# First block's gates as pairs of column chunks with seven-product units, and another order of the bank reads at the ends of output pairs

## The chip, the cores and the metric

One core of one Trainium2 chip. The metric is the device time of one execution in microseconds (us), given as the median of three runs.

## The reference

Two transformer-like blocks run one after the other on an activation of 256 tokens by 2048 channels, in fp32. What the change touches:

```python
# first block
proj = rms_norm(x, norm_mix_g) @ w_in              # the last 4 * 2048 columns are the gates
gates = sigmoid(gate_logits.reshape(b, s, 4, d))   # one gate of 2048 columns for each of four branches
branches = einsum('bskw,kwd->bskd', ys, w_branch)
merged = sum(gates * branches, axis=2)
x = x + merged @ w_out
x = x + square(relu(rms_norm(x, norm_mlp_g) @ w_mlp_up)) @ w_mlp_down
# second block
...
x = x + (silu(h2 @ w_gate) * (h2 @ w_up)) @ w_down
```

## The kernel before

**Products.** Every large product is fp32 made of three passes of a reduced type (fp32r): each operand is split into a high half (a rounded copy) and a low half (the rest), and high x high, low x high and high x low are added in PSUM. ACT makes the high half of the weights (`hi_unit`, L422), DVE the low half (`lo_unit`, L430), both for a unit of 1 MB. Weights pass through a ring of four raw slots and two split slots. A unit is four k-tiles by 512 columns; with two row tiles of 128 tokens it has 24 matmuls of 512 columns (`unit_products`, L433 to L456): sixteen that need the high half, then eight that need the low half. Semaphores order everything: `hi_split` and `lo_split` count halves of units, `units_used` the units that PE has done. ACT makes the high half of a unit when PE has done the unit two before; SP loads a unit when the low half of the one three before is made.

**Order.** PE runs 76 groups of four units and then the units of the pairs of the second block. Groups 8 to 11 are the gates of four branches for the first chunk of 512 columns, group 12 the four branch products for it. Groups 13 to 27 are three turns of five groups for the other three chunks (`gate_turn`, L1673): one group for each branch's gate, accumulated in `acc[:, k % 2]`, and one group of four branch units. ACT turns a gate into a sigmoid when its group is done (`evac`, L958), while PE works in the other half of `acc`. DVE multiplies gate and branch (`branch_part`, L2171, instruction L2182) and POOL adds the four results (`merge`, L899). Turned matrices pass through the PSUM tile `tp` (L500) on the way to the output product. Groups 28 to 31 are w_out, 32 to 35 the first up product.

**Pairs.** From group 36 on, three times, come two output pairs ("scaled") and four up groups; the second block's MLP consists of pairs too: 11 of gate and up, 6 of down. A pair works on two chunks of columns at once, so on all four banks of `acc` (chunk b, row tile m). Its unit is two k-tiles by two chunks: a 2 x 2 x 2 product of blocks. Units 3 and 5 (in the first down pairs others) are done with seven products instead of eight, by sums of blocks: `seven_low` and `seven_high` make the sums of weight blocks and split them (DVE L2272 to L2286, ACT L987 to L992), `operand_sums` and `operand_low` (L2289 to L2310) with `sums_high` (L994) make those of the other operand, once for an operand. `seven_products` (L1743) has 21 matmuls. Three of the seven products go to banks of their own in `sd` and `tp`; `combine` (L2325) makes vw and yz from them after the last seven unit and q_sum is copied by ACT (`q_copy`, L1003). `plain_products` (L1706) does the first and the last unit of a pair bank by bank: in the first it waits for each bank to be free (`bank_free`, L1691), does four matmuls, waits for the whole low half, and does two more. In the last each bank reports when it is done (`bank_done`).

**Ends of output pairs.** After the first unit's split of the next pair (or the up group), DVE runs `finish_scaled` (L2378): the two banks of chunk 0 into xres (`bank_to_x`, L2350), then the combined sums into xres (`sums_to_x`, four operations at L2364), then the two banks of chunk 1. In the second block `finish_first` and `finish` (L2596, L2605) do the same with L2352 and L2371 to L2375. After a gate pair the first addition (L2603) is made before the next unit's split already.

Of the kernel before, what the change touches and what calls it, by code (L numbers as in the profile page):

```python
# [110 lines left out]
FIRST_SEVEN, QUARTERS = (3, 5), 3  # L111

# [13 lines left out]
def build(nc, t, out):  # L126

    ctx = ExitStack()
    with ctx:
# [132 lines left out]
        t_sum = at("t_sum", 160, [P, 4, NW])  # L262
# [3 lines left out]
        a_full = at("a_full", 164, [P, 2, T])  # L266
        a_sum = at("a_sum", 166, [P, 4, P])
# [4 lines left out]
        q_sums = [at("q_sum", 148, [P, NW]), at("q_sum2", c0 + 1.5, [P, NW])]  # L272
# [83 lines left out]
        q_copied = sem("q_copied")  # L356
        combined, silu_in, hidden2 = sem("combined"), sem("silu_in"), sem("hidden2")
# [28 lines left out]
        w_dn = rows_of(t["w_mlp_down"][0])  # L386
        conv_cols = t["w_in_2"][0][:, I2_B0:I2_B0 + 2 * W].rearrange("(k p) (v f n) -> p k v f n", p=P, v=2, f=2)
# [11 lines left out]
        def loads_before(group):  # L399

            return group + min(max(group - G_HEAD2, 0), 2) + max(group - G_PAIR0, 0)
# [134 lines left out]

        PAIRS1 = [Pair(n, "scaled", (G_DLOOP + 8 * (n // 2)) * UN + n % 2 * PAIR_UNITS, PAIR_UNITS, FIRST_SEVEN, 1,
# [14 lines left out]
        for p in PAIRS1 + PAIRS:  # L552
            ahead = PAIRS1[:p.n] if p.kind == "scaled" else PAIRS1 + PAIRS[:p.n]
            p.order = len(ahead)
            p.combined = sum(3 if q.kind == "gate" else 6 for q in ahead)
# [3 lines left out]
            p.q_sum = q_sums[p.kind != "scaled"]  # L559
# [11 lines left out]
        SUMS1 = 2 * QUARTERS  # L571
# [7 lines left out]
        SUM_LOWS = [last_seven(PAIRS1[2 * i], 0) for i in range(QUARTERS) for _ in range(2)]  # L579
# [6 lines left out]
        def sums_made(p, v):  # L586

            x = p.places.index(v)
            if p.kind == "scaled":
                return 2 * p.chunk[0] + x + 1  # L590
            return SUMS1 + (x + 1 if p.op == 0 else 3 + 2 * p.chunk[0] + x)

# [102 lines left out]
        def _(sp):  # L695
# [262 lines left out]
        def _(act):  # L958
# [22 lines left out]
            def seven_high(p, v):  # L981
# [8 lines left out]
                act.activation(seven_hi[:, 3:5, :], t_sum[:, 0:2, :], ACT.Copy)  # L990
                act.wait_ge(t_made, 3 * n + 3)
                act.activation(seven_hi[:, 5:7, :], t_sum[:, 2:4, :], ACT.Copy).then_inc(hi_split, 1)  # L992
# [5 lines left out]
            def first_sums_high(i, j):  # L998

                if j in (1, 3):  # L1000
                    sums_high(1, j // 2, 2 * i + j // 2)
# [1670 lines left out]
```

## Time and profile before

| | us |
|---|---|
| median of 3 runs (2473.68 to 2473.72) | 2473.7 |
| the profiled execution | 2474.51 |
| its span, first to last instruction | 2472.8 |
| PE busy | 2453.8 |
| PE weight loads busy | 2047.9 |
| DVE busy | 1708.5 |
| ACT busy | 1212.2 |
| POOL busy | 116.6 |

Matmuls are pipelined: one of 512 columns is shown with some 390 ns, though the next starts some 227 ns after it. So the pace is read from starts, not from durations. The waits view names for each idle time of an engine the instruction that ended it. In a timeline row stand start, duration, engine, line, operation, output and inputs, a count where neighbours are merged, and in brackets the idle time before it and what ended it.

### The profile page before, as it was taken

To read this page: it belongs to the slowest core of one execution; us is meant where nothing else is said; L and a number is where in the kernel's file an instruction comes from. 1 tells how busy PE (TensorE), PEld (TensorE's weight loads), DVE (VectorE), ACT (ScalarE), POOL (GpSimd) and SP (SyncE) were. 2 spreads that over 40 slices of the span, in tenths; PEclk is the share of its full clock that TensorE was granted. 3 is DMA by queue.
4 is the path that set the end of the run, shared out by engine and by line. 5 is a ranking of instruction groups with operands and counts; after the bars stand their busy time and mean duration, and the time that the engine had idled before them with its cause. 6 is when DMAs were issued, how large, how long until landed. Compare 5 with 4: busy or idle time off the path is not lost.

```text
span 2472.8 us, 28758 instructions
## 1 busy us (share of the span) xinstructions
PE 2453.8 (99%) x11719; PEld 2047.9 (83%) x11719; DVE 1708.5 (69%) x1590; ACT 1212.2 (49%) x1270; POOL 116.6 (5%) x95
## 2 busy tenths in 40 slices
PE   9999999999999999999999999999999999999999
PEld 8888888888888878888888888788888788878887
DVE  5775455454655785776765558886788878887887
ACT  5545534343344444544444448875555444544553
POOL 0410010010110000000000010000200000000000
PEclk9999999999999999999999999999999999999999
DMA  7555465666655565655665655444556565655654
GB/s 252 173 184 180 160 192 192 196 194 196 230 184 187 187 201 188 197 192 175 201 194 192 209 171 189 153 151 162 180 191 199 190 194 185 207 195 191 203 187 153
DMA packets 233138, 467.18 MB, mean 189 GB/s; under 512 B 13424, under 2 KB 25216, under 8 KB 232622
## 3 DMA queue, kind: packets, MB, share of 16 engines
q1 hardware_dynamic: 231454, 460.09, 57.4%
q10 hardware_dynamic: 1552, 5.25, 0.6%
q8 instruction: 93, 1.52, 0.3%
q14 instruction: 39, 0.32, 0.0%
HBM read 463.20 MB, written 2.10 MB: 188 GB/s over the span
## 4 chain that ended last, share of the span: by engine, by line
PE 93%; DVE 4%; ACT 1%; issue 1%; POOL 0%; DMA 0%; ACTq 0%; DVEq 0%; POOLq 0%
PE acc L445 13%; PE acc L454 13%; PE acc L447 13%; PE acc L1714 9%; PE acc L1715 9%; PE acc L1718 9%; PE acc L474 5%; PE acc L480 2%; PE sd L474 2%; PE tp L474 2%; DVE wlo L430 1%; PE tp L480 1%; PE sd L480 1%; PE acc L1772 1%; PE acc L1768 1%; PE acc L1769 1%
## 5 line engine op out<-in xcount | busy, mean ns | idle before, releaser
L430 DVE TENSOR_TENSOR wlo<-raw,whi 128x2048 fp32r<-128x2048 f32 (+1 forms) x396 | 913.5, 2308 | 642.9 <-ACT whi L422 641.8
L422 ACT ACTIVATE whi<-raw 128x2048 fp32r<-128x2048 f32 (+1 forms) x396 | 748.0, 1890 | 844.4 <-PE acc L454 356.4
L445 PE MATMUL acc<-whi,opA_hi 128*128 128x512 f32 x1152 | 454.8, 395 | 0.0
L447 PE MATMUL acc<-whi,opA_lo 128*128 128x512 f32 x1152 | 449.4, 390 | 0.0
L454 PE MATMUL acc<-wlo,opA_hi 128*128 128x512 f32 x1152 | 287.4, 391 | 0.2 <-DVE wlo L430 0.2
L445 PEld LDWEIGHTS acc<-whi,opA_hi 128*128 128x128 f32 x1152 | 216.9, 188 | 45.4 <-issue 0.9
L447 PEld LDWEIGHTS acc<-whi,opA_lo 128*128 128x128 f32 x1152 | 216.8, 188 | 44.2
L454 PEld LDWEIGHTS acc<-wlo,opA_hi 128*128 128x128 f32 x1152 | 214.9, 188 | 44.8 <-DVE wlo L430 0.8
L1714 PE MATMUL acc<-whi,opA_hi 128*128 128x512 f32 x552 | 216.0, 391 | 5.9 <-DVE xres L2350 3.8
L1715 PE MATMUL acc<-whi,opA_lo 128*128 128x512 f32 x552 | 215.0, 389 | 0.0
L1714 PE MATMUL acc<-whi,opB 128*128 128x512 f32 x536 | 209.7, 391 | 1.4 <-DVE xres L2352 1.4
L1715 PE MATMUL acc<-whi,opB 128*128 128x512 f32 x536 | 208.7, 389 | 0.0
L474 PE MATMUL acc<-opB,whi 128*128 128x512 f32 x512 | 159.2, 392 | 1.1 <-DVE xres L2350 1.1
L445 PE MATMUL acc<-whi,opB 128*128 128x512 f32 (+1 forms) x384 | 147.5, 387 | 2.0 <-ACT whi L422 2.0
L1718 PE MATMUL acc<-wlo,opA_hi 128*128 128x512 f32 x552 | 148.1, 389 | 0.0
L447 PE MATMUL acc<-whi,opB 128*128 128x512 f32 (+1 forms) x384 | 145.1, 381 | 0.0
L1718 PE MATMUL acc<-wlo,opB 128*128 128x512 f32 x536 | 143.1, 389 | 0.0
L1714 PEld LDWEIGHTS acc<-whi,opA_hi 128*128 128x128 f32 x552 | 103.6, 188 | 30.4 <-DVE xres L2350 5.0
L1718 PEld LDWEIGHTS acc<-wlo,opA_hi 128*128 128x128 f32 x552 | 103.6, 188 | 21.7
L1715 PEld LDWEIGHTS acc<-whi,opA_lo 128*128 128x128 f32 x552 | 103.7, 188 | 21.0
L1714 PEld LDWEIGHTS acc<-whi,opB 128*128 128x128 f32 x536 | 100.6, 188 | 23.1 <-DVE xres L2352 2.2
L1718 PEld LDWEIGHTS acc<-wlo,opB 128*128 128x128 f32 x536 | 100.6, 188 | 20.9
(417 smaller groups left out, 3373.9 us busy)
## 6 DMA issues: line engine op xcount, KB each, us to landing
raw<-in_w_in SPq DMA_DIRECT2D x114, 1024.0 KB, 5.4
raw<-in_w_mlp_up SPq DMA_DIRECT2D x64, 1024.0 KB, 5.5
raw<-in_w_mlp_down SPq DMA_DIRECT2D x64, 1024.0 KB, 5.0
raw<-in_w_gate SPq DMA_DIRECT2D x88, 512.0 KB, 3.8
raw<-in_w_up SPq DMA_DIRECT2D x88, 512.0 KB, 4.7
raw<-in_w_down SPq DMA_DIRECT2D x88, 512.0 KB, 4.7
raw<-in_w_out SPq DMA_DIRECT2D x32, 1024.0 KB, 5.0
raw<-in_w_branch SPq DMA_DIRECT2D x16, 1024.0 KB, 5.0
```

The costliest lines, as they stand in the source:

```text
L422: eng.activation(whi[:, j % SPL, k, 0:cols], raw[:, j, k, 0:cols], ACT.Copy).then_inc(hi_split, share(k))
L430: eng.tensor_tensor(wlo[:, j % SPL, k, 0:cols], raw[:, j, k, 0:cols], whi[:, j % SPL, k, 0:cols].bitcast(F32), ALU.subtract).then_inc(lo_s ...
L445: eng.matmul(acc[:, pair, m, 0:cols], hi[:, kt + i, m * P:(m + 1) * P], whi[:, s, i, 0:cols], start=first and i == 0, stop=False)
L447: eng.matmul(acc[:, pair, m, 0:cols], lo[:, kt + i, m * P:(m + 1) * P], whi[:, s, i, 0:cols], start=False, stop=False)
L454: mm = eng.matmul(acc[:, pair, m, 0:cols], hi[:, kt + i, m * P:(m + 1) * P], wlo[:, s, i, 0:cols], start=False, stop=last and i == UK - 1)
L474: eng.matmul(up_bank(group, c), whi[:, s, i, c * P:(c + 1) * P], opB[:, UK * j + i, :, :].rearrange("p v t -> p (v t)"), start=j == 0 and ...
L480: mm = eng.matmul(up_bank(group, c)[:, 0:T], wlo[:, s, i, c * P:(c + 1) * P], opB[:, UK * j + i, 0, :], start=False, stop=j == UN - 1 and ...
L1714: pe.matmul(acc[:, b, m, :], hi[:, 2 * v + a, rows], whi[:, s, 2 * a + b, :], start=first and a == 0, stop=False)
L1715: pe.matmul(acc[:, b, m, :], lo[:, 2 * v + a, rows], whi[:, s, 2 * a + b, :], start=False, stop=False)
L1718: return pe.matmul(acc[:, b, m, :], hi[:, 2 * v + a, m * P:(m + 1) * P], wlo[:, s, 2 * a + b, :], start=False, stop=last and a == 1)
L1768: pe.matmul(bank, a_h, seven_hi[:, i, :], start=alone and first, stop=False)
L1769: pe.matmul(bank, a_l, seven_hi[:, i, :], start=False, stop=False)
```

## The change

- `PAIRS0`: the gates of the last three chunks (groups 13 to 16, 18 to 21, 23 to 26) become six pairs. The even pair of a turn holds branches 0 and 1, the odd pair branches 2 and 3; the two "chunks" of a pair are the same 512 columns of two branches. Units 3 and 5 of each have seven products. Each unit is loaded by two transfers of 512 KB, one a branch.
- DVE adds the combined sums to the four banks in place (`sum_gates`), then ACT makes four sigmoids (`sigmoids`). After an even pair DVE adds to bank (0,0) before the next split and to the three others after it; after an odd pair to the two banks of b=0 before the split and to the two of b=1 after it.
- The sums of the operand (the normalised input) are made in group 12, in between the branch products of the first chunk: the operand sums at its units 0 and 2, their low halves at 1 and 3.
- At the ends of output pairs bank (0,0) (before an up group both banks of b=0) is read into xres before the next unit's split, the other banks after it, and `sums_to_x` comes behind the second unit's split. `finish_scaled` is gone.
- PE's first seven unit of a pair waits only until the pair before has been combined (`sums_read`), not until its sums are in xres.
- Tiles for sums and copies have new places, and what counts pairs, sums and loads is shifted by the six pairs.

```diff
+BRANCH_SEVEN, LATER = (3, 5), 3
...
+        PAIRS0 = [Pair(n, "sigmoid", (G_LOOP + 5 * (n // 2) + 2 * (n % 2)) * UN, PAIR_UNITS, BRANCH_SEVEN, 1,
+                       BRANCH_SEVEN, (n // 2, n % 2), 0) for n in range(2 * LATER)]
...
+            p.sums_read = ahead[-1].combined + 3 if ahead else 0
...
# SP
-                for k in range(NB):
-                    for j in range(UN):
-                        load_unit(sp, G_LOOP + k + i * 5, j, w_in, UK * j, i * NW + (IN_GATE + k * D + NW))
+                for p in PAIRS0[2 * i:2 * i + 2]:
+                    for v in range(p.units):
+                        u = p.unit + v
+                        sp.wait_ge(lo_split, (u - RAW + 1) * HV)
+                        to = raw[:, u % RAW].rearrange("p (a b) c -> p a b c", a=2)
+                        for b in range(2):
+                            sp.dma_start(to[:, :, b, :], gate_cols[:, 2 * v:2 * v + 2, 2 * p.chunk[1] + b, chunk(i + 1)]
+                                         ).then_inc(landed[u % RAW], 16)
...
# ACT
+            def sigmoids(p):
+                for b in range(2):
+                    for m in range(MT):
+                        act.wait_ge(gate_summed, 4 * p.n + 2 * b + m + 1)
+                        act.activation(gates[:, 2 * p.chunk[1] + b, m, :], acc[:, b, m, :], ACT.Sigmoid,
+                                       scale=rstd[:, m:m + 1]).then_inc(read_act, 1)
...
             def gate_turn(i, last=False):
...
+                for p in PAIRS0[2 * i:2 * i + 2]:
+                    for v in range(p.units):
+                        if v in p.seven:
+                            seven_high(p, v)
+                        else:
+                            hi_unit(act, (p.unit + v) // UN, v % UN)
+                        if p.chunk[1] and v == 0:
+                            sigmoids(PAIRS0[p.n - 1])
+                        if v == p.units - 1:
+                            q_copy(p)
+                for j in range(UN):
+                    hi_unit(act, G_LOOP + NB + i * 5, j)
+                    if j == 0:
+                        sigmoids(PAIRS0[2 * i + 1])
...
# PE
+                if p.kind == "sigmoid":
+                    if p.chunk[1]:
+                        pe.wait_ge(read_act, readers_before(R_LOOP + 2 * NB * p.chunk[0], "A") * MT + 2 * b + m + 1)
+                    else:
+                        pe.wait_ge(read_dve, readers_before(R_LOOP + 2 * NB * p.chunk[0] - 1 + b, "D") * MT)
...
-                        pe.wait_ge(combined, p.combined)
+                        pe.wait_ge(combined, p.sums_read)
...
+                for p in PAIRS0[2 * i:2 * i + 2]:
+                    for v in range(p.units):
+                        (seven_products if v in p.seven else plain_products)(p, v, opA_hi, opA_lo)
...
# DVE
+            def sum_gates(p, banks):
+
+                for b, m in banks:
+                    bank_wait(p, b, m)
+                    if b:
+                        dve.wait_ge(combined, p.combined + 3)
+                    src = yz[:, m, :] if b else vw[:, 1, :] if m else p.q_sum[:, :]
+                    dve.tensor_tensor(acc[:, b, m, :], acc[:, b, m, :], src,
+                                      ALU.subtract if (b, m) == (0, 1) else ALU.add).then_inc(gate_summed, 1)
...
                     branch_part(0, j - 1, R_GATE0 + NB + j - 1, dve_g * UN + j)
+                if j % 2:
+                    operand_low(1, j // 2, j // 2)
+                else:
+                    operand_sums(1, BRANCH_SEVEN[j // 2], j // 2, 0)
...
+                        if p.chunk[1] and v == 0:
+                            sum_gates(PAIRS0[p.n - 1], [(0, 0)])
+                        if v in p.seven:
+                            seven_low(p, v)
+                        else:
+                            lo_unit(dve, (p.unit + v) // UN, v % UN)
+                        if p.chunk[1] and v == 0:
+                            sum_gates(PAIRS0[p.n - 1], [(0, 1), (1, 0), (1, 1)])
+                        if p.chunk[1] == 0 and v == 0:
+                            branch_part(i, NB - 1, R_LOOP - 1, i * (5 * UN) + G_LOOP * UN, i)
+                        if v == p.units - 1:
+                            combine(p)
+                for j in range(UN):
+                    if j == 0:
+                        sum_gates(PAIRS0[2 * i + 1], [(0, 0), (0, 1)])
+                    lo_unit(dve, G_LOOP + NB + i * 5, j)
+                    if j == 0:
+                        sum_gates(PAIRS0[2 * i + 1], [(1, 0), (1, 1)])
...
# DVE, scaled pairs
+                        if p.chunk[1] and v == 0:
+                            banks_to_x(PAIRS1[p.n - 1], lambda b, m: (b, m) == (0, 0))
                         if v in p.seven:
                             seven_low(p, v)
...
                         if p.chunk[1] and v == 0:
-                            finish_scaled(PAIRS1[p.n - 1])
+                            banks_to_x(PAIRS1[p.n - 1], lambda b, m: (b, m) != (0, 0))
+                        if p.chunk[1] and v == 1:
+                            dve.wait_ge(read_dve, read_first(p))
+                            sums_to_x(PAIRS1[p.n - 1])
...
+                        if c == 0 and j == 0:
+                            banks_to_x(PAIRS1[2 * i + 1], lambda b, m: b == 0)
                         lo_unit(dve, g, j)
                         if c == 0 and j == 0:
-                            finish_scaled(PAIRS1[2 * i + 1])
+                            banks_to_x(PAIRS1[2 * i + 1], lambda b, m: b == 1)
+                        if c == 0 and j == 1:
+                            dve.wait_ge(read_dve, read_first(PAIRS1[2 * i + 1]) + 2 * MT)
+                            sums_to_x(PAIRS1[2 * i + 1])
...
# DVE, pairs of the second block
                 if p.kind == "down":
                     bank_to_x(p, 0, 1)
-                    if p is not PAIRS[-1]:
-                        dve.wait_ge(bank_read, 4 * p.n + MT)
-                        sums_to_x(p)
                     for m in range(MT):
                         bank_to_x(p, 1, m)
                     return
...
-                    if v == 0 and p.n and PAIRS[p.n - 1].kind == "gate":
+                    if v == 0 and p.n:
                         finish_first(PAIRS[p.n - 1])
                     if v in p.seven:
                         seven_low(p, v)
                     else:
                         lo_unit(dve, (p.unit + v) // UN, (p.unit + v) % UN)
-                    if v == 0 and p.n and PAIRS[p.n - 1].kind == "down":
-                        finish_first(PAIRS[p.n - 1])
+                    if v == 1 and p.n and PAIRS[p.n - 1].kind == "down":
+                        dve.wait_ge(bank_read, 4 * p.n)
+                        sums_to_x(PAIRS[p.n - 1])
```

## Rows read from the trace of the kernel before

**Rows 1.** The page: its head, and the busy time of each engine.
```profile
span 2472.8 us, 28758 instructions
...
PE 2453.8 (99%) x11719; PEld 2047.9 (83%) x11719; DVE 1708.5 (69%) x1590; ACT 1212.2 (49%) x1270; POOL 116.6 (5%) x95
```
**Rows 2.** Waits of PE: who waited for whom, us in total, times, longest.
```profile
PE acc L1714 <- DVE xres L2350: 3.8, 3, 1.3
PE acc L1714 <- DVE xres L2352: 3.5, 5, 0.7
...
PE acc L474 <- DVE xres L2350: 1.1, 3, 0.4
...
PE sd L1772 <- DVE seven_lo L2282: 0.5, 1, 0.5
```
**Rows 3.** Timeline of PE: starts of a plain, a seven-product and a plain unit.
```profile
846.85 0.39 PE L1714 MATMUL acc<-whi,opA_hi 128*128 128x512 f32 x1
...
852.29 0.39 PE L1768 MATMUL sd<-seven_hi,opA_hi 128*128 128x512 f32 x1
...
857.05 0.39 PE L1714 MATMUL acc<-whi,opA_hi 128*128 128x512 f32 x1
```
**Rows 4.** Timeline of DVE at the end of a gate pair, second block.
```profile
1838.75 0.69 DVE L2603 TENSOR_TENSOR acc<-acc,q_sum 128x512 f32<-128x512 f32 x1
1839.39 2.29 DVE L430 TENSOR_TENSOR wlo<-raw,whi 128x2048 fp32r<-128x2048 f32 x1
```
**Rows 5.** Timeline from 316 to 326 us: POOL, DVE, PE.
```profile
316.18 2.40 POOL L899 TENSOR_TENSOR xres<-xres,stage 128x1024 f32<-128x1024 f32 x1 [133.39 <-DVE stage L2182]
...
316.91 3.82 DVE L430 TENSOR_TENSOR wlo<-raw,whi 128x2048 fp32r<-128x2048 f32 x1 [0.81 <-ACT whi L422]
...
322.35 4.19 DVE L430 TENSOR_TENSOR wlo<-raw,whi 128x2048 fp32r<-128x2048 f32 x1 [0.42 <-ACT whi L422]
...
323.68 1.98 PE L454 MATMUL acc<-wlo,opB 128*128 128x512 f32 x8
```
**Rows 6.** Timeline of DVE: first and last of the five operand sums.
```profile
817.11 0.69 DVE L2299 TENSOR_TENSOR a_full<-opA_hi,opA_lo 128x512 f32<-128x512 f32 x1
...
818.69 0.29 DVE L2304 TENSOR_TENSOR a_sum<-a_full,a_sum 128x128 f32<-128x128 f32 x1
```
**Rows 7.** Timeline of POOL and DVE near 120 us.
```profile
118.97 4.43 POOL L874 TENSOR_TENSOR lru_g<-lru_g,lru_u 128x1024 f32<-128x1024 f32 x1
...
121.06 3.42 DVE L2122 SCALAR_TENSOR_TENSOR lru_p<-lru_p,lru_z 128x1024 f32<-128x1024 f32 x1
```
**Rows 8.** Timeline of PE: first unit of an odd scaled pair, start, wait, next start.
```profile
878.13 0.44 PE L1714 MATMUL acc<-whi,opA_hi 128*128 128x512 f32 x1
...
882.35 0.50 PE L1714 MATMUL acc<-whi,opA_hi 128*128 128x512 f32 x1 [1.27 <-DVE xres L2350]
...
885.20 0.39 PE L1714 MATMUL acc<-whi,opA_hi 128*128 128x512 f32 x1
```
**Rows 9.** Timeline of DVE at the same place.
```profile
873.20 1.22 DVE L2338 TENSOR_TENSOR yz<-vw,sd 128x1024 f32<-128x1024 f32 x1
874.99 2.29 DVE L430 TENSOR_TENSOR wlo<-raw,whi 128x2048 fp32r<-128x2048 f32 x1 [0.57 <-ACT whi L422]
877.20 1.40 DVE L2350 SCALAR_TENSOR_TENSOR xres<-acc,smalls,xres 128x512 f32<-128x512 f32 x2
...
881.54 1.41 DVE L2350 SCALAR_TENSOR_TENSOR xres<-acc,smalls,xres 128x512 f32<-128x512 f32 x2
```
**Rows 10.** Timeline of PE: last unit of an odd scaled pair into the up group.
```profile
921.47 0.61 PE L1718 MATMUL acc<-wlo,opA_hi 128*128 128x512 f32 x2
922.45 0.73 PE L474 MATMUL acc<-opB,whi 128*128 128x512 f32 x2 [0.37 <-DVE xres L2350]
```
**Rows 11.** Timeline of PE: first unit behind a down pair, second block.
```profile
2170.70 0.50 PE L1714 MATMUL acc<-whi,opA_hi 128*128 128x512 f32 x1 [0.70 <-DVE xres L2352]
```
**Rows 12.** The page's DMA issues: KB each, median us from issue to landing.
```profile
raw<-in_w_up SPq DMA_DIRECT2D x88, 512.0 KB, 4.7
```

More of the change, by code:

```diff
@@ L399, in loads_before @@
         def loads_before(group):
-            return group + min(max(group - G_HEAD2, 0), 2) + max(group - G_PAIR0, 0)
+            gates_ = sum(min(max(group - p.unit // UN, 0), 2) for p in PAIRS0)
+            return group + gates_ + min(max(group - G_HEAD2, 0), 2) + max(group - G_PAIR0, 0)
         def parts(group):
@@ L551, in build @@
                 unit += size * CT // 2
-        for p in PAIRS1 + PAIRS:
-            ahead = PAIRS1[:p.n] if p.kind == "scaled" else PAIRS1 + PAIRS[:p.n]
+        EVERY = PAIRS0 + PAIRS1 + PAIRS
+        for p in EVERY:
+            ahead = EVERY[:EVERY.index(p)]
             p.order = len(ahead)
-            p.combined = sum(3 if q.kind == "gate" else 6 for q in ahead)
+            p.combined = sum(3 if q.kind in ("gate", "sigmoid") else 6 for q in ahead)
+            p.sums_read = ahead[-1].combined + 3 if ahead else 0
             p.gates = sum(q.kind == "gate" for q in ahead)
@@ L2256, in add_to_x @@
-            def add_to_x(run, n, done):
-                dve.wait_ge(units_used, done)
-                for m in range(MT):
-                    dve.tensor_tensor(xres[:, m, chunk(n)], acc[:, run % 2, m, :], xres[:, m, chunk(n)],
-                                      ALU.add).then_inc(read_dve, 1)
             def seven_low(p, v):
@@ L2331, in combine @@
                     dve.wait_ge(combined, n)
-                if p.n and p.kind != "scaled":
+                if p.n and p.kind == "sigmoid":
+                    dve.wait_ge(gate_summed, 4 * p.n)
+                elif p.n and p.kind != "scaled":
                     dve.wait_ge(bank_read, 4 * p.n)
@@ new lines, in gate_turn @@
+            def gate_turn(i, last=False):
+                for p in PAIRS0[2 * i:2 * i + 2]:
+                    for v in range(p.units):
+                        if p.chunk[1] and v == 0:
[10 more added lines that the diff above has]
+                            combine(p)
+                for j in range(UN):
+                    if j == 0:
[3 more added lines that the diff above has]
+                        sum_gates(PAIRS0[2 * i + 1], [(1, 0), (1, 1)])
+                    if last and j >= 2:
+                        merged_lo(j - 2)
+                    if j:
+                        branch_part(i + 1, j - 1, R_LOOP + NB + j - 1, i * (5 * UN) + (G_LOOP + NB) * UN + j, i + 1)
@@ new lines, in _, with hidden_squares @@
+            for i in range(2):
+                gate_turn(i)
+            gate_turn(2, last=True)
+            def hidden_squares(run, group):
+                pair = (group - 1) % 2
+                for h, banks in enumerate((acc[:, pair], (sd, tp)[pair])):
+                    dve.wait_ge(hidden_low, run * 2 + h + 1)
+                    dve.tensor_tensor(hidT[:, 2 * h:2 * h + 2, :], banks[:, :, 0:T], hid_low[:, 2 * h:2 * h + 2, :],
+                                      ALU.add).then_inc(read_dve, 1)
+                for h in range(2):
+                    x = hidT[:, 2 * h:2 * h + 2, :]
+                    dve.wait_ge(read_dve, (readers_before(R_UP0 + run_of(run), "D")) * MT + h + 1)
+                    dve.scalar_tensor_tensor(x, x, 0.0, x, ALU.max, ALU.mult).then_inc(hidden_ready, 1)
```

213 lines of the change are left out of this document (97 added, 116 removed).

## The prediction

> **What bounds the kernel.** The page first: PE is busy 2453.8 us of a span of 2472.8 us [rows 1], so time is bought with fewer matmuls or with less waiting in front of them. The waits of PE come next [rows 2]: its largest are 3.8 us behind L2350 (three times), 3.5 us behind L2352 (five times) and 1.1 us behind L2350 (three times, ahead of L474). These are DVE's reads of the accumulation banks at the ends of output pairs. Last, the pace of PE in its timeline [rows 3]: a plain unit of a pair (24 matmuls of 512 columns) goes from 846.85 to 852.29, 5.44 us or 0.2267 us a matmul; the seven-product unit after it (21 matmuls) goes from 852.29 to 857.05, 4.76 us. A unit of seven saves 0.68 us of the engine that bounds.
>
> **Part 1, the gates as pairs.** Six pairs with two units of seven each: 12 x 0.68 = **8.2 us less**. The other units keep 24 matmuls. The four operand sums are made once, from the normalised input, and serve all six pairs.
>
> What is added lies on DVE and ACT: per seven unit 6 DVE operations, about 6.6 us together against 2.3 us for a plain split; per pair a combine (three operations, about 2.6 us), four additions and four sigmoids (two more than a branch had). A pair's DVE work is then some 6 x 2.3 + 2 x 6.6 + 2.6 + 2.7 + 1.3 = 34 us in the 42 us that PE needs for it. It fits on the average; what counts is the order at the ends.
>
> *Even pair to odd pair.* Count from E, the end of the pair's last unit as the other engines see it. The gate pairs of the second block have this order today: the combine, one addition into bank (0,0), the next split, the rest [rows 4]. The addition starts at 1838.75, 4 us before the end of its pair, the split at 1839.39, and [rows 2] has no row for PE behind L2603, L2616 or the silu, over 11 pairs. In the new pairs all four banks pass through an addition and then a sigmoid. By the same durations the additions end at E-3.3, -0.3, +0.4 and +1.1, the sigmoids at -2.6, +0.4, +1.1 and +1.8; PE wants the banks at about E-0.2, +1.2, +2.5 and +3.9. All are in time, by 0.8 us at the least: cost 0. If the additions were later by more than that, PE would pay the difference.
>
> *Odd pair to branch group.* Both b=0 banks are added before the split: sigmoids done by E-1.3, wanted at E-0.2. The split of the first branch unit ends at E+0.3 and is wanted at E+3.4; the second unit's high half starts behind the sigmoids at E+2.4, ends at +4.3 and is wanted at +5.2. Cost 0. The merging in the third turn comes up to 1.1 us later in its first step and has caught up at its third.
>
> *Branch group to even pair.* Here something is in the way. POOL adds xres and stage for 2.40 us at 316.18; the split that starts at 316.91 takes 3.82 us, and the next 4.19 us, where it takes 2.29 us alone [rows 5]: while one of them runs, the other stands. That long split ends at 326.54. The last branch unit's lows start at 323.68, eight matmuls, so the next unit starts at 325.49. As a plain group it wants its low half after 16 matmuls, at 329.1. As the first unit of a pair, which goes bank by bank, it wants it after four: 326.4. The split is late by 0.14 us, with the semaphore and the slow restart about 0.3 us. The second and third turns have the same operations at the same distances (4.19 us again): **0.6 us for both**.
>
> In the first turn this group carries the operand sums too: 817.11 to 818.98, 1.9 us [rows 6], then a low part of 0.7 us. The second set (j=2) comes at 316.1 exactly as POOL starts. The first sum gets in, POOL goes next to 319.0, the rest ends at 320.1, the split of the fourth unit at 322.4 (wanted at 323.5), branch_part at 323.6. POOL is due then, but the low part holds DVE to 324.2. Who goes next, the waiting POOL or the split behind it on DVE? [rows 7] answer: POOL L874 has waited from 118.97, DVE goes from L430 to L2122 at 121.06, and L2122 takes 3.42 us for 1024 elements: the waiting POOL went first. So POOL runs to 326.4, the split to 328.7, and PE stands 328.7 - 326.4 = 2.3 us, 2.4 us with the restart. If DVE went first it would be 0.5 us; if both sets were late behind POOL, 4 us. I take **2.4 us**, since [rows 7] are the same two engines in the same state.
>
> **Part 2, the borders of output pairs.** At the even-odd border of the scaled pairs the first unit goes from 878.13 to 885.20, 7.07 us instead of 5.44, with 1.27 us of idle at 882.35 behind L2350 [rows 8]. DVE shows why [rows 9]: combine done at 874.42, then 0.57 us of waiting, split 874.99 to 877.20, two bank reads to 878.60, then sums_to_x (about 3 us) and only at 881.54 the banks b=1. PE wants the third bank at about 880.9. In the new order bank (0,0) is read in the gap before the split (it is ready at about E-4, as in [rows 4]), the split ends at about 877.4, three reads end at 878.2, 878.9 and 879.6. Wanted: 879.5, 880.9, 882.2. The 1.6 us go, three times: **4.8 us**. sums_to_x comes behind the second unit's split, 882.7 to 885.7; the third unit's split then ends at 888.1 and is wanted near 892.7. The combined sums are free for the next pair's sevens once combine has run, so their wait is shorter too.
>
> Into the up group, L474 starts at 922.45 where the two lows from 921.47 would let it start at 921.92 [rows 10]: 0.5 us and 0.1 us of restart, three times: **1.9 us**. With the two reads ahead of the split it ends at 922.4, wanted at 925.5.
>
> Second block: 0.70 us of idle at 2170.70 behind L2352 [rows 11]; with the slow matmuls around it ([rows 8] lose 1.63 us for 1.27 us of idle) about 1.0 us, five times: **5.0 us**. The wait behind seven_lo L2282 in [rows 2] (0.5 us, with restart 0.8 us) comes at 1926.99, after such a border whose second unit is of seven: DVE came late to it because of sums_to_x. That now stands behind it: **0.8 us**. In the same pair a seven unit follows three units on with only 0.5 us to spare on DVE, so half a microsecond can come back.
>
> **The sum.** 8.2 + 4.8 + 1.9 + 5.0 + 0.8 = 20.7 us less; 0.6 + 2.4 = 3.0 us more: 17.7 us. The profiled execution took 2474.51 us (span 2472.8 us), 0.8 us above the median of 2473.7 us; a difference carries over. 2473.7 - 17.7 = **2456.0 us**. Bounds: DVE first at POOL's lock and no small losses 2454; borders at their bare idle (3.8 + 3.5 + 1.1 + 0.5 instead of 12.5 us) 2460; own range 2453 to 2460.
>
> **Rivals.**
> *The borders keep a wait.* The bank read ahead of the split costs the split 0.7 us and ties it to the combine; if the split came behind the fourth matmul, each of eight borders would keep about 1 us: 2464 us. [rows 4] speak against it (that order, no wait). 0.08.
> *The gate stage keeps DVE late.* After the 2.4 us stall, or next to POOL, a seven unit or an end of a pair loses 1 us in each of six pairs: 2462 us. For it: more DVE work per unit than before in this stage. Against it: 8 us of slack per pair. 0.08.
> *The loads land late, and it is slower.* The pair units are loaded as two transfers of 512 KB instead of one of 1024 KB. A load is issued when the split three units before is done, and its high half must be ready for PE some 17 us later, less 2 us for ACT: cover 15 us. A transfer of 512 KB lands in 4.7 us [rows 12]; two, even one after the other, in 9.4 us. From 15 us on each of 48 units pays: at 16 us 48 us, so 2504 us. It is slower than before by over 0.2% once the lateness passes 22.6/48 = 0.5 us. Chance 0.02. The Trainium skill (SBUF — State Buffer, "The DMA setup-cost knee") speaks against the change here: it asks for the largest single transfer, as each pays about 2 us whatever its size. As an estimate from that page each unit's load would take 2 us longer. The trace shows the second block loading this way with PE never behind a weight load [rows 2], so its rule would move nothing unless the cover were gone.
> *Nothing comes.* The removed matmuls are not on the path or the stalls move to the next wait of equal size: 2473 us. Against 99% busy. 0.02.
>
> **The numbers.** Forecast 0.80, rivals 0.08, 0.08, 0.02, 0.02. Range 2452.5 to 2463: it holds the forecast and about half of the first two rivals. 0.2% is 4.9 us, about what a measurement of this kernel can tell from no change: faster 0.95, same 0.03, slower 0.02.
>
> **What would show it.** PE's matmuls 36 fewer by the products (12 x 3); the three rows of PE behind L2350 and L2352 gone; seven units of 4.76 us between 325 and 625 us; one new wait of PE on L430 of about 2 us near 326 us and two of 0.2 us about 108 us apart after it. The first block's gate stage should shorten by about 5 us, the scaled stage by 6.7 us, the second block by 5.8 us. The forecast is wrong if PE shows waits behind the sigmoids or the additions, or if ACT or DVE wait for landings.

## The result and the profile after

The changed kernel takes 2455.8 us (median of five runs) against 2473.7 us: the ratio is 0.9929 with a 95% interval of [0.9914, 0.9944]. It is 17.9 us faster; the forecast was 17.7. One of the five executions took 2789.5 us at a mean granted clock of 0.82 and does not enter the ratio; the other four lie between 2455.7 and 2456.6 us. The total fits better than its parts do, as the stages show. The profiled execution took 2456.6 us (span 2454.8 us), 0.8 us above the median.

The page of the changed kernel, its first lines and two of its DMA issues (columns as in [rows 12]):

```profile
span 2454.8 us, 28949 instructions
...
PE 2442.9 (100%) x11683; PEld 2042.7 (83%) x11683; DVE 1791.8 (73%) x1704; ACT 1236.9 (50%) x1314; POOL 117.0 (5%) x95
...
raw<-in_w_in SPq DMA_DIRECT2D x66, 1024.0 KB, 5.3
...
raw<-in_w_in SPq DMA_DIRECT2D x120, 512.0 KB, 4.7
```

PE has 11683 matmuls, 36 fewer than in [rows 1], as 12 units of seven make it. The new gate loads of 512 KB (96 of the 120 in the last row) land in 4.7 us; no wait of PE leads back to them.

The waits of PE in the changed kernel (waiting operation, what released it: us in total, times, longest):

```profile
PE acc L450 <- ACT whi L427: 2.0, 3, 1.1
PE acc L1741 <- DVE wlo L435: 1.9, 1, 1.9
PE sd L1672 <- POOL ones L850: 1.2, 1, 1.2
PE tp L1867 <- ACT q2T L1344: 0.8, 1, 0.8
PE tp L505 <- POOL stage L929: 0.7, 1, 0.7
```

Lines have moved: the split L430 is now L435, the conversion L422 is L427, the pairs' matmuls L1714, L1715 and L1718 are L1737, L1738 and L1741, the bank reads L2350 and L2352 are L2322 and L2324, branch_part is L2226. Against [rows 2], the three rows behind the bank reads are gone, and so is the one behind seven_lo. Only the row of L1741 is new. It is the first matmul with a low half in the first gate pair. PE's timeline there (start, duration, instruction, idle time before it with its releaser):

```profile
324.77 0.39 PE L1738 MATMUL acc<-whi,opA_lo 128*128 128x512 f32 x1
327.01 0.74 PE L1741 MATMUL acc<-wlo,opA_hi 128*128 128x512 f32 x2 [1.86 <-DVE wlo L435]
...
328.34 0.63 PE L1738 MATMUL acc<-whi,opA_lo 128*128 128x512 f32 x1
...
329.62 0.63 PE L1737 MATMUL acc<-whi,opA_hi 128*128 128x512 f32 x1
330.05 0.63 PE L1738 MATMUL acc<-whi,opA_lo 128*128 128x512 f32 x1
...
331.94 0.39 PE L1737 MATMUL acc<-whi,opA_hi 128*128 128x512 f32 x1
...
435.07 0.73 PE L1741 MATMUL acc<-wlo,opA_hi 128*128 128x512 f32 x2
...
541.49 0.73 PE L1741 MATMUL acc<-wlo,opA_hi 128*128 128x512 f32 x2
```

DVE and POOL beside it, each from its own timeline:

```profile
320.67 1.28 DVE L2226 TENSOR_TENSOR stage<-acc,gates 128x512 f32<-128x512 f32 x2
321.87 0.68 DVE L2278 TENSOR_TENSOR ad_lo<-a_sum,ad_hi 128x512 fp32r<-128x512 f32 x1
322.47 4.49 DVE L435 TENSOR_TENSOR wlo<-raw,whi 128x2048 fp32r<-128x2048 f32 x1
...
322.03 2.78 POOL L919 TENSOR_TENSOR xres<-xres,stage 128x1024 f32<-128x1024 f32 x1 [4.48 <-DVE stage L2226]
```

This is the forecast's first turn, in the forecast's order: POOL falls due at 322.03 while the low half of the operand sums (L2278) holds DVE, POOL goes next and ends at 324.81, and the split behind it on DVE, issued at 322.47, ends only at 326.96 (4.49 us for what takes 2.29 alone). PE idles 1.86 us. The other two turns lose 0.20 us each: the start before 435.07 is 434.64, 0.43 us instead of 0.23, and the same at 541.49. So small a wait does not appear among the waits.

One thing was not in the forecast. From 328.34 to 331.94 the matmuls start 0.43 us apart, not 0.227. The windows of that stretch (busy us of PE, PEld, DVE, ACT and POOL with the number of instructions, then granted clock, DMA share, GB/s):

```profile
324.00:327.00 3.00, 1.16 (x6) 0.61 (x4) 3.00 (x2) 1.92 (x1) 0.81 (x1) 1.00 0.49 191
327.00:328.70 1.70, 1.69 (x6) 1.38 (x7) 1.70 (x3) 0.00 (x0) 0.46 (x1) 0.86 0.22 22
328.70:332.00 3.30, 3.30 (x10) 2.59 (x9) 1.66 (x1) 0.00 (x0) 3.30 (x1) 0.55 0.97 320
332.00:336.00 4.00, 4.00 (x19) 3.31 (x18) 0.38 (x1) 2.40 (x3) 0.59 (x1) 1.00 0.70 251
```

The granted clock is 0.55 for 3.3 us, near the lower of its two levels (1.2 instead of 2.4 GHz), and then 1.00 again. Some eight matmuls are 0.20 us late each: 1.6 us.

At a border between even and odd scaled pairs DVE now shows this ([rows 9] are the same place before):

```profile
868.11 1.22 DVE L2310 TENSOR_TENSOR yz<-vw,sd 128x1024 f32<-128x1024 f32 x1
869.25 0.74 DVE L2322 SCALAR_TENSOR_TENSOR xres<-acc,smalls,xres 128x512 f32<-128x512 f32 x1
869.91 2.28 DVE L435 TENSOR_TENSOR wlo<-raw,whi 128x2048 fp32r<-128x2048 f32 x1
872.11 2.06 DVE L2322 SCALAR_TENSOR_TENSOR xres<-acc,smalls,xres 128x512 f32<-128x512 f32 x3
...
875.33 2.29 DVE L435 TENSOR_TENSOR wlo<-raw,whi 128x2048 fp32r<-128x2048 f32 x1 [1.17 <-ACT whi L427]
877.54 0.75 DVE L2336 SCALAR_TENSOR_TENSOR xres<-q_sum,smalls,xres 128x512 f32<-128x512 f32 x1
```

The first bank read fills the gap that [rows 9] have before the split, the other three follow at once and end at 874.17, and the sums come behind the next unit's split. There is still 1.17 us of slack ahead of that split.

The stages, from starts of PE's matmuls in each profile (gate stage: first gate pair or group 13 to the first matmul of w_out; scaled stage: its first pair to the first matmul of group 60; second block: its first pair to the last matmul of the kernel):

| us | start of group 12 | gate stage | scaled stage | second block's pairs |
|---|---|---|---|---|
| before | 303.73 | 329.78 | 527.06 | 713.10 |
| after | 302.33 | 326.08 | 520.16 | 707.13 |
| difference | -1.40 | -3.70 | -6.90 | -5.97 |
| forecast | 0 | -5.2 | -6.7 | -5.8 |

The forecast row holds the terms of the prediction's sum, 5.2 for the gate stage being 8.2 less 3.0. The differences sum to 17.97 us, all of the span's 18.0. The start (everything before group 12, untouched by the change) is 1.4 us shorter, and the gate stage gained 1.5 us less than forecast: two things outside the forecast that cancel in these two profiles. The experiments had to say whether either belongs to the change.

### The profile page after: what moved, and what is told of

It is laid out like the page before. It is cut to its first block, busy times and chain, and to the rows that moved or that the text cites. A ratio compares the mean times of both kernels' runs of the same rounds, so it can differ in the third digit from the quotient of the medians.

```text
span 2454.8 us, 28949 instructions
## 1 busy us (share of the span) xinstructions
PE 2442.9 (100%) x11683; PEld 2042.7 (83%) x11683; DVE 1791.8 (73%) x1704; ACT 1236.9 (50%) x1314; POOL 117.0 (5%) x95
## 4 chain that ended last, share of the span: by engine, by line
PE 96%; DVE 2%; ACT 1%; issue 1%; POOL 0%; DMA 0%; ACTq 0%; DVEq 0%; POOLq 0%
PE acc L1741 13%; PE acc L1737 13%; PE acc L1738 13%; PE acc L459 10%; PE acc L450 10%; PE acc L452 10%; PE acc L479 5%; PE acc L485 2%; PE tp L479 2%; PE sd L479 2%; PE acc L1795 2%; PE acc L1792 2%; PE acc L1791 2%; PE sd L485 1%; PE tp L485 1%; PE sd L1795 1%
## 5 line engine op out<-in xcount | busy, mean ns | idle before, releaser
L435 DVE TENSOR_TENSOR wlo<-raw,whi 128x2048 fp32r<-128x2048 f32 (+1 forms) x384 | 884.8, 2305 | 538.9 <-ACT whi L427 537.9
L427 ACT ACTIVATE whi<-raw 128x2048 fp32r<-128x2048 f32 (+1 forms) x384 | 724.9, 1889 | 795.5 <-PE acc L1741 339.2
L1737 PE MATMUL acc<-whi,opA_hi 128*128 128x512 f32 x840 | 327.7, 390 | 0.0
L1738 PE MATMUL acc<-whi,opA_lo 128*128 128x512 f32 x840 | 327.6, 390 | 0.0
L450 PE MATMUL acc<-whi,opA_hi 128*128 128x512 f32 x768 | 304.6, 397 | 0.0
L452 PE MATMUL acc<-whi,opA_lo 128*128 128x512 f32 x768 | 299.4, 390 | 0.0
L1741 PE MATMUL acc<-wlo,opA_hi 128*128 128x512 f32 x840 | 226.0, 390 | 1.9 <-DVE wlo L435 1.9
L1737 PE MATMUL acc<-whi,opB 128*128 128x512 f32 x536 | 209.5, 391 | 0.0
L1738 PE MATMUL acc<-whi,opB 128*128 128x512 f32 x536 | 208.6, 389 | 0.0
L459 PE MATMUL acc<-wlo,opA_hi 128*128 128x512 f32 x768 | 192.6, 392 | 0.2 <-DVE wlo L435 0.2
L1741 PEld LDWEIGHTS acc<-wlo,opA_hi 128*128 128x128 f32 x840 | 158.1, 188 | 36.0 <-DVE wlo L435 3.2
L1738 PEld LDWEIGHTS acc<-whi,opA_lo 128*128 128x128 f32 x840 | 158.0, 188 | 32.7
L1737 PEld LDWEIGHTS acc<-whi,opA_hi 128*128 128x128 f32 x840 | 158.0, 188 | 32.7
L450 PEld LDWEIGHTS acc<-whi,opA_hi 128*128 128x128 f32 x768 | 144.3, 188 | 30.2 <-issue 0.9
L452 PEld LDWEIGHTS acc<-whi,opA_lo 128*128 128x128 f32 x768 | 144.3, 188 | 29.0
L459 PEld LDWEIGHTS acc<-wlo,opA_hi 128*128 128x128 f32 x768 | 142.8, 188 | 29.8 <-DVE wlo L435 0.8
L1741 PE MATMUL acc<-wlo,opB 128*128 128x512 f32 x536 | 143.1, 389 | 0.0
L2253 DVE TENSOR_TENSOR seven_lo<-t_sum,seven_hi 128x2048 fp32r<-128x2048 f32 x56 | 127.9, 2284 | 0.0
L1741 PEld LDWEIGHTS acc<-wlo,opB 128*128 128x128 f32 x536 | 100.6, 188 | 20.9
```

Source lines behind the costliest of these rows:

```text
L427: eng.activation(whi[:, j % SPL, k, 0:cols], raw[:, j, k, 0:cols], ACT.Copy).then_inc(hi_split, share(k))
L435: eng.tensor_tensor(wlo[:, j % SPL, k, 0:cols], raw[:, j, k, 0:cols], whi[:, j % SPL, k, 0:cols].bitcast(F32), ALU.subtract).then_inc(lo_s ...
L450: eng.matmul(acc[:, pair, m, 0:cols], hi[:, kt + i, m * P:(m + 1) * P], whi[:, s, i, 0:cols], start=first and i == 0, stop=False)
L452: eng.matmul(acc[:, pair, m, 0:cols], lo[:, kt + i, m * P:(m + 1) * P], whi[:, s, i, 0:cols], start=False, stop=False)
L459: mm = eng.matmul(acc[:, pair, m, 0:cols], hi[:, kt + i, m * P:(m + 1) * P], wlo[:, s, i, 0:cols], start=False, stop=last and i == UK - 1)
L1737: pe.matmul(acc[:, b, m, :], hi[:, 2 * v + a, rows], whi[:, s, 2 * a + b, :], start=first and a == 0, stop=False)
```

## The experiments

**1. The borders alone.** The kernel before, with only the new order at the ends of output pairs.

```
+ banks_to_x(PAIRS1[p.n - 1], lambda b, m: (b, m) == (0, 0))   # ahead of the first split
  ...
- finish_scaled(PAIRS1[p.n - 1])
+ banks_to_x(PAIRS1[p.n - 1], lambda b, m: (b, m) != (0, 0))   # behind it
+ if p.chunk[1] and v == 1:
+     dve.wait_ge(read_dve, read_first(p))
+     sums_to_x(PAIRS1[p.n - 1])
  ...
- pe.wait_ge(combined, p.combined)
+ pe.wait_ge(combined, p.sums_read)
```

> The kernel before with the new order of the bank reads and sums at the ends of output pairs, and nothing else. Theory (the two parts are independent, the ends cost 12.5 us before): 2473.7 - 12.5 = 2461.2 us, scaled stage 6.9 us shorter, pairs of the second block 6.0 us shorter, no wait of PE behind the xres reads. Rival (part of what the changed kernel won at the ends comes from the shift in time that the gate pairs bring): less than 11 us.

Measured: 2461.1 us, ratio 0.9949 [0.9935, 0.9962]; scaled stage 520.16, second block 707.09, gate stage 329.76 as before. The borders are worth 12.4 us by medians, 12.9 us by stages. No wait behind a bank read is left: the rival in which the read ahead of the split costs each border 1 us is out.

**2. The gates alone.** The changed kernel with the old borders (the reverse of the edit above).

> The changed kernel with the old order at the ends of output pairs. Theory: the gate stage alone wins 8.2 us of matmuls and gives back some 4.5 us, so 2473.7 - 3.7 = 2470.0 us; the waits behind the xres reads are back (8.4 us idle). Rival (the 17.9 us are mostly the gates and the ends were hidden): 2463 us or less.

Measured: 2469.3 us, ratio 0.9982 [0.9973, 0.9991], an effect of 4.4 us, where [0.9973, 0.9991] allows 2.2 to 6.7. The gate stage is 324.42, 5.36 us shorter; the scaled stage is as before (527.03), the second block 0.2 us longer (713.33). Its waits of PE have the old rows again, to the tenth as in [rows 2]:

```profile
PE acc L1737 <- DVE xres L2322: 3.8, 3, 1.3
PE acc L1737 <- DVE xres L2324: 3.5, 5, 0.7
PE acc L450 <- ACT whi L427: 1.9, 3, 1.1
PE acc L1741 <- DVE wlo L435: 1.9, 1, 1.9
PE sd L1672 <- POOL ones L850: 1.2, 1, 1.2
PE acc L479 <- DVE xres L2322: 1.1, 3, 0.4
```

The gate stage has the same idle of 1.85 us in front of L1741, but the window behind it shows no slow clock:

```profile
328.00:332.00 4.00, 3.95 (x17) 3.30 (x18) 3.39 (x3) 0.00 (x0) 2.73 (x1) 1.00 0.66 208
```

So the slow matmuls are 1.6 us that this idle can bring, not that it always brings. Without them the gate stage gains what the forecast said.

**3. Which half of the new border does it?** The changed kernel with all four bank reads behind the split again, in the old order of banks; only the sums stay behind the second unit's split.

```
- banks_to_x(PAIRS1[p.n - 1], lambda b, m: (b, m) == (0, 0))
  ...
- banks_to_x(PAIRS1[p.n - 1], lambda b, m: (b, m) != (0, 0))
+ banks_to_x(PAIRS1[p.n - 1], lambda b, m: True)
  ...  # the same ahead of the up group and behind the down pairs
```

> The changed kernel, but all bank reads of an output pair come behind the next unit's split as before; only the combined sums are moved behind the second unit's split. Theory: at the even-odd ends and in the second block PE waited for the banks b=1 behind the sums, so moving the sums alone takes those waits away (3 x 1.6 + 5 x 1.0 us); what stays is the end into the up group, where both banks of b=0 are wanted at once: 3 x 0.6 us, so about 2457.7 us. Rival (bank (0,0) in the gap ahead of the split is what matters): the eight other ends keep 0.5 us or more each, 2462 us.

Measured: 2458.7 us, ratio 0.9939 [0.9926, 0.9951]. Its waits of PE behind bank reads:

```profile
PE acc L479 <- DVE xres L2322: 1.1, 3, 0.4
```

The eight waits of 0.7 to 1.3 us at the ends of even scaled pairs and down pairs stay away with the sums moved alone. The three ahead of the up group come back; the scaled stage is 2.3 us longer (0.76 each) and the second block 0.6 us. Moving the sums (with PE's earlier start of the seven units, which stays in this kernel) is worth about 10 of the 12.9 us; reading banks ahead of the split, on top of it, gives the rest. What the reads ahead of the split would give without the move, no run shows. The forecast of this run was 1.0 us too low: 0.76 us for each up group instead of 0.6, and the 0.6 us of the second block.

**4. Is the start part of the change?** The kernel before once more.

> The kernel before, unchanged, for one more profiled execution: is the start (first matmul of group 12 at 303.73 us before, 302.33 us after the change) a matter of the execution or of the change? Theory (execution): 302.3 to 303.8 us again, and if it is 302.3 the span is about 2471.4 us. Rival (the change): 303.7 us.

Measured: group 12 starts at 302.33, the same as in the changed kernel's profile, and stages are 329.78, 527.03 and 713.02. The start belongs to the execution, not to the kernel: over all profiles it lies between 302.3 and 303.7. In this one PE runs 23 matmuls from 8 to 12 us, in the first profile of the kernel before 15: there the matmuls start 0.43 us apart up to 10.5 us, here 0.23. The windows of both give a granted clock of 1.00 for that stretch, so they do not tell why. The span is 2471.2 us, 2471.4 had been expected.

**5. The changed kernel again.**

> The changed kernel once more, for its profile: its wait of 1.9 us near 326 us is followed by eight matmuls at 0.427 us in the profile at hand, by none in the two experiments with the same wait (gates alone, sums later alone). Theory (the wait is of a length at which the clock falls in some executions and not in others): either is possible, and the gate stage is 326.1 us with slow matmuls, 324.4 us without. Rival (something of the changed kernel itself slows these matmuls): 326.1 us again.

Measured: gate stage 324.47 with the same idle of 1.86 us, and then:

```profile
328.70:332.00 3.30, 3.30 (x16) 2.71 (x15) 1.72 (x1) 0.00 (x0) 3.30 (x1) 1.00 0.95 312
```

16 matmuls in that window at a clock of 1.00, where the first profile had 10 at 0.55, with POOL busy all through it and 312 GB/s moved, as there. Neither explains the slow stretch.

**6. Take the low half out of POOL's way.** In the first gate pair the second set's low half comes behind the second unit's split, so that DVE is free when POOL falls due.

```
- if j % 2:
-     operand_low(1, j // 2, j // 2)
+ if j == 1:
+     operand_low(1, 0, 0)
  ...
+ if p.n == 0 and v == 1:
+     operand_low(1, 1, 1)
```

> The changed kernel with one DVE operation of 0.7 us moved: the low half of the second operand sums comes behind the split of the second unit of the first gate pair instead of ahead of the first unit's. Theory (lock between DVE and POOL, waiting POOL goes first; then a slow clock after a long idle): the split now starts right behind branch_part, ahead of POOL, and takes 2.3 instead of 4.5 us; PE's idle of 1.9 us and the eight slow matmuls behind it (1.6 us) both go: 2455.8 - 3.6 = 2452.2 us. Rival (DVE is only late by its queue): the wait gets shorter by 0.7 us, 2455.0 us. Second rival (the slow matmuls come from DMA or POOL beside PE, not from the idle): 2453.8 us with slow matmuls left near 329 us.

Measured: 2454.0 us, ratio 0.992 [0.9907, 0.9934]; gate stage 323.56, a gain of 0.9 us on 324.47 where 2 was expected. DVE, POOL and PE, each from its timeline:

```profile
322.96 2.28 DVE L435 TENSOR_TENSOR wlo<-raw,whi 128x2048 fp32r<-128x2048 f32 x1
...
327.63 1.29 DVE L2226 TENSOR_TENSOR stage<-acc,gates 128x512 f32<-128x512 f32 x2 [2.39 <-POOL xres L919]
...
323.12 4.38 POOL L919 TENSOR_TENSOR xres<-xres,stage 128x1024 f32<-128x1024 f32 x1 [4.48 <-DVE stage L2226]
...
328.98 0.50 PE L1737 MATMUL acc<-whi,opA_hi 128*128 128x512 f32 x1 [0.92 <-DVE stage L2226]
```

The split wins by 0.16 us and takes its 2.28 us. Now POOL is the one held up: 4.38 us instead of 2.40. branch_part, which writes the buffer that POOL reads, waits 2.39 us for it, and PE waits 0.92 us for the bank that branch_part reads. That the two engines hold each other up is shown from both sides, and half of the gain became a new wait one step on. That part of the expectation fell.

**7. The small waits of the other turns.** As 6, and PE takes the first unit of an even gate pair two banks at a time, so that it wants the low half after 8 matmuls, not 4.

```
+ if first and p.kind == "sigmoid" and p.chunk[1] == 0:
+     for b in range(2):
+         ...  # bank_free and high for m = 0, 1
+         pe.wait_ge(lo_split, (u + 1) * HV)
+         ...  # low for m = 0, 1
```

> The kernel before this one in the list, and the first unit of an even gate pair done two banks at a time: low half wanted after eight matmuls instead of four. Theory: the two late splits of the second and third turn (0.2 us each in the changed kernel's profile) are covered: 0.4 to 0.6 us less, 2451.7 us. Rival (the banks b=1, read by branch_part behind the late split, become the wait): no difference or slower by some tenths.

Measured: gate stage 322.84, 0.72 us shorter: 0.34 us in each of the two turns and 0.04 in the first, which keeps its wait of 0.9 us. The median is 2453.7 us, ratio 0.9919 [0.9906, 0.9933] (6 had 2454.0); that difference is inside the noise, the stages show the gain.

**8. What an idle of PE costs.** As 6, with n more operand sums on DVE ahead of the third unit's split in the second gate pair, where POOL is idle.

```
+ if p.n == 1 and v == 2:
+     for _ in range(n):
+         own.done(dve.tensor_tensor(a_fulls[0][:, :, :], opA_hi[:, 0:2, :].bitcast(F32), ...))
```

With n = 10:

> The kernel with the low half later, and ten operand sums of 0.73 us (repeated, the result unused) on DVE ahead of one split, that of the third unit of the second gate pair, where POOL does nothing: a dose of idle for PE. DVE has about 6.0 us to spare there, so PE should stand about 1.3 us. Theory (the clock follows the idle time): after 1.3 us the pace stays 0.227 us a matmul, as after the 1.27 us of the kernel before; the kernel is 1.4 us longer than the one without. Rival (slow matmuls come from traffic beside PE): the same here; the next kernel tells.

With n = 12:

> The same with twelve operations: PE should stand about 2.8 us. Theory (clock follows idle): matmuls at 0.427 us for some us behind it, 8 or more of them, so the kernel is 4.5 us or more longer than the one without. Rival (traffic of DMA and POOL beside PE near 329 us was the cause): the pace stays 0.227 us and the kernel is 2.8 us longer.

PE's timeline with n = 10:

```profile
383.78 2.11 PE L1741 MATMUL acc<-wlo,opA_hi 128*128 128x512 f32 x8 [0.79 <-DVE wlo L435]
385.73 0.40 PE L1791 MATMUL sd<-seven_hi,opA_hi 128*128 128x512 f32 x1
...
388.11 0.50 PE L1795 MATMUL sd<-seven_lo,opA_hi 128*128 128x512 f32 x1 [0.84 <-DVE seven_lo L2249]
```

and with n = 12:

```profile
385.24 3.63 PE L1741 MATMUL acc<-wlo,opA_hi 128*128 128x512 f32 x8 [2.24 <-DVE wlo L435]
388.70 0.39 PE L1791 MATMUL sd<-seven_hi,opA_hi 128*128 128x512 f32 x1
```

with the windows of n = 12:

```profile
385.20:388.80 3.60, 3.56 (x9) 2.85 (x10) 3.53 (x5) 2.06 (x2) 0.00 (x0) 0.54 0.64 196
389.00:393.00 4.00, 4.00 (x19) 3.30 (x18) 4.00 (x3) 1.90 (x1) 0.00 (x0) 1.00 0.24 70
```

Each kernel was executed once, in 2457.1 us (n = 10) and 2459.2 us (n = 12). The idle ahead of L1741 came out about half a microsecond shorter than expected in both, and with n = 10 a second one of 0.84 us follows in the next unit. After these two idles the pace is unchanged (8 matmuls in 1.95 us) and the gate stage is 2.24 us longer than in 6, where 1.4 was expected. After an idle of 2.24 us the same eight take 3.46 us at a granted clock of 0.54, and the stage is 4.04 us longer: 2.24 us and a restart, and 1.6 us again for slow matmuls. POOL does nothing in that window, and 196 GB/s are moved in it, less than the 312 GB/s of experiment 5 at full clock. So the slow stretch is the doing neither of POOL nor of the traffic.

The lists of all executions say the same. Each has its mean granted clock; in the profiles it is 0.999 with a slow stretch and 1.000 without. Of the 21 executions of the kernels with the 1.86 us idle (the changed kernel without the execution at 0.82, and experiments 2, 3 and 5) 8 have 0.999. Of the 58 listed of kernels without it (the kernel before, experiments 1, 6, 7, 9 and 10, and n = 10) none has; the one with n = 12 has 0.999. Those 8 are by their medians only 0.5 us (experiment 2) to 1.1 us (experiment 3) longer than the others of their kernel, so the 1.6 us of the two traces is not confirmed by them.

**9. Sums first.** Both sets of operand sums stand in the first unit of group 12, with a buffer more for the second; its low half precedes the second branch_part. ACT makes both high halves in the second unit.

```
+ if j == 2:
+     operand_low(1, 1, 1)
  branch_part(...)
  ...
+ if j == 0:
+     operand_sums(1, BRANCH_SEVEN[0], 0, 0)
+     operand_sums(1, BRANCH_SEVEN[1], 1, 0)
+ elif j == 1:
+     operand_low(1, 0, 0)
```

> The changed kernel with both sets of operand sums made in the first unit of group 12, before POOL has anything to do (a second buffer for the sums), and the second low half ahead of the second branch_part, in an idle microsecond of DVE. Theory (what is late in the first turn is only the 2.6 us of operand work beside POOL): the first turn looks like the two later ones, 0.2 us of idle behind the split and none behind branch_part: gate stage 322.4 us, the kernel about 2453.0 us. Rival (POOL and DVE collide in the first gate pair anyway): a wait of 0.9 us or more stays near 326 us, as in the version with only the low half moved.

Measured: 2453.7 us, ratio 0.9919 [0.9906, 0.9933]; gate stage 322.60. DVE and POOL are back at the durations of [rows 5]:

```profile
315.94 3.82 DVE L435 TENSOR_TENSOR wlo<-raw,whi 128x2048 fp32r<-128x2048 f32 x1 [0.82 <-ACT whi L427]
...
321.38 4.19 DVE L435 TENSOR_TENSOR wlo<-raw,whi 128x2048 fp32r<-128x2048 f32 x1 [0.42 <-ACT whi L427]
```

and the first turn loses what the others lose. The gate stage is 1.87 us shorter than the 324.47 of experiment 5: the price of having the sums beside POOL.

**10. Both.** Experiments 9 and 7 together.

> The same with the first unit of an even gate pair two banks at a time. Theory: nothing is left of the waits at the starts of the three even gate pairs; gate stage 321.7 us, which is the old 329.8 less 8.2 us; the kernel about 2452.4 us, the best of all versions. Rival: the banks b=1 become the wait (branch_part ends 2.2 us after the start of the unit, they are wanted after 2.7 us), some tenths each turn.

Measured: 2452.9 us, ratio 0.9915 [0.9902, 0.9929], against a kernel before of 2473.3; gate stage 321.61. That is 329.78 less 8.17, the whole of 12 x 0.68: nothing is lost at the three turns. Its page:

```profile
span 2451.4 us, 28949 instructions
...
PE 2441.7 (100%) x11683; PEld 2042.9 (83%) x11683; DVE 1790.6 (73%) x1704; ACT 1236.5 (50%) x1314; POOL 116.6 (5%) x95
```

It is the fastest of all by median, 2.9 us below the changed kernel (20.4 us against 17.9 us, each against the kernel before as executed beside it). The intervals of the two ratios overlap; what shows the gain is the gate stage, 2.9 us shorter than the changed kernel's at full clock (324.47) with the other stages equal to 0.03 us.

## Why the prediction was right

*The matmuls.* 12 x 0.68 = 8.2 us: experiment 10 shows 8.17. With full additions and sigmoids at the ends of pairs, DVE and ACT never held PE; the forecast's zero there stood.

*Even scaled pair to odd pair, odd pair to up group.* Forecast 4.8 and 1.9 us, measured together 6.90 us. Experiment 3 divides it nearly as the forecast did: the sums' move carries the first (4.6 us), the reads ahead of the split the second (2.3 us, so 0.4 us more than given).

*Second block.* Forecast 5.0 + 0.8 us, measured 5.97. The half microsecond that could have come back at a seven unit did not: no wait on seven_lo is left. The step that charged more for a stall than its idle time was needed: bare idle alone (8.9 us of rows) would have missed a third of the 12.9. Its size was right, its reason only in part. The prediction speaks of slow matmuls around the stall. The timeline of PE in the kernel before, at the wait of [rows 8] (the matmul at 882.35), shows two other things:

```profile
880.46 0.61 PE L1718 MATMUL acc<-wlo,opA_hi 128*128 128x512 f32 x2
...
882.68 0.39 PE L1715 MATMUL acc<-whi,opA_lo 128*128 128x512 f32 x1
```

The idle of 1.27 us is counted from 881.07, where the second matmul of the first line is shown to end, 0.39 us after its start. By the usual pace the next would have started 0.23 us after it, at 880.91: 0.16 us of the stall are not in its idle time. The first matmul behind the stall then takes 0.34 us to the next start instead of 0.23. In experiment 8 the same shows: two idles of 0.79 and 0.84 us made the stage 2.24 us longer, 0.3 us more for each.

*The first turn.* Forecast 2.4 us, measured 2.2 us at full clock (1.87 from experiment 9 to the changed kernel's second profile, and 0.33 of the 0.99 us that 10 has on 9). The reading of [rows 7], that the waiting POOL goes ahead of the next operation on DVE, was right. Experiment 6 showed how near the other order was: with DVE 0.16 us ahead it is POOL that waits.

*The other turns.* Forecast 0.3 us each, measured 0.34 (experiment 7) and 0.33 (10 against 9).

*The loads.* Landing 4.7 us with a cover estimated at 15: no wait. The rule of the Trainium skill (SBUF — State Buffer, "The DMA setup-cost knee") to coalesce into the largest single transfer moved nothing here, as the forecast had it.

*What the sum did not have.* The slow matmuls behind the first turn's idle, 1.6 us, in one execution of the changed kernel and not in the next; and the length of the start, which varies by 1.4 us with no change. In the two profiles compared first they cancelled, and that their difference of 18.0 us lies so near the forecast is luck to that extent. Without both, the stages give 5.3 + 6.9 + 6.0 = 18.2 us against 17.7: the terms of the borders were 0.4 us low, the losses of the gate stage 0.1 us high. The median difference, 17.9 us, lies between.

The rivals: waits at the borders are out by experiment 1, lateness in the gate stage by the waits of the changed kernel, late landings by the page, and no effect by the result.

## What to carry over

A border between output groups is paid by the operation that stands between the last matmul and the next split: take out of it everything that frees no bank (here the sums, 10 of 12.9 us), then put into the gap ahead of the split what is ready. Where DVE and POOL hold each other up, an operation added on DVE at the moment when POOL falls due lets POOL in ahead of the split behind it; place it where POOL is idle (1.9 us for a move of some lines, experiment 9). Read single stages over several executions before crediting a matching total to the parts.

## What the runs showed of the hardware

*DVE's split and POOL's addition hold each other up whole.* Whichever of the two is first runs at its own length; the other stands until it is done and then needs its own length: the split 4.49 us with POOL ahead, POOL 4.38 us with the split ahead (2.29 and 2.40 alone). A lead of 0.16 us decided. When POOL had been waiting during one operation of DVE it went before the next, although that was queued directly behind (322.03 and 322.47 us in the changed kernel).

*A short idle can halve the matmul clock afterwards.* Over these profiles the lower level came after an idle of 2.24 us (one of one) and after 1.86 us in one of four profiled executions with the same instructions (8 of 21 by the granted clocks of all executions); after 0.79 us, and after 1.27 us in the kernel before ([rows 8]: the 12 matmuls from the restart to the next unit take 2.85 us, the usual pace and 0.1 us for the restart), no such stretch followed. In the two traces it cost some eight matmuls at 0.43 instead of 0.227 us, 1.6 us on top of the idle. The Trainium skill (TensorE: Matmul & The Clock Gate, "HAM oscillation — how this bites in real kernels") also ties the lower clock to idle gaps of the engine; the trace agrees, with the 2.24 us and the 0.54 of experiment 8, but the idles that did it here are shorter than the gaps of that section, and the measurement decides. Why the same idle brings it in one execution and not in another stays open.

*The idle time of the waits view is less than a stall costs.* Each stall of PE in this stream of 512-column matmuls took 0.3 us more than its idle time (1.63 for 1.27 us, 2.24 for 0.79 + 0.84 us).

*The start varies.* Before group 12 the same instructions took 302.3 to 303.7 us from one execution to another, with more or fewer matmuls at 0.43 us near 8 to 10 us. It is about as large as the effect that was missing in the gate stage of the first profile, and hid it in the total.
